# Half groups of weight matmuls moved into waiting places, two products laid side by side in 64 output rows, and one set of scores formed on VectorE

## The chip, the cores and the metric
The kernel runs on one core of one Trainium2 chip (trn2), in one launch. The metric is device microseconds. Everything is float32. Each `matmul` of the program is two MATMUL records in the trace and each transpose one, so a row that says x8 on PE is four matmuls or eight transposes.

## The reference, cut to what matters
One inference step of a 2-layer decoder trunk for a prompt of 256 tokens and 8 sample tokens that share all weights. Each layer has a mixer of three branches, merged by gates, and then a feed-forward part:

```python
z = h @ w_in                                   # one wide input projection
# branch A: gated DeltaNet in 2 chunks of 128;  branch C: mLSTM, same chunks
# branch B: latent attention
c_kv = rmsnorm(b_ckv, mla_kv_norm_g)           # latent of the newest tokens
k_rope = rope(b_kr, pos)                       # rotary key: x*cos + swapped x*(+-sin)
k_nope = einsum('bsc,chd->bshd', c_kv, w_uk)   # prompt keys of 8 heads
q_lat = einsum('bqhd,chd->bqhc', q_nope, w_uk) # sample queries in latent space
s_past = q_lat . lat_past + q_rope . kr_past   # against 2048 cached tokens a sample
s_new  = q_lat . c_kv     + q_rope . k_rope    # against the newest token: 8 samples x 8 heads
merged = g_a*(o_a @ w_branch_a) + g_b*(o_b @ w_branch_b) + g_c*(o_c @ w_branch_c)
x += merged @ w_out;   x += down(silu(conv(gate)) * up)
```

## The kernel before
Activations stay in SBUF as 128 channels x 264 tokens (256 prompt + 8 sample). Weights stream from HBM through a ring of 8 slots (SyncE issues the loads; a slot holds 8 tiles of 128x128). Nearly all of TensorE's time is `weights()` (line 546): one 128x128 tile times 264 columns. The five engines run their own written-out instruction lists and meet through semaphores.

The order on TensorE is written by hand. Some weight products depend on little and can be done at any time; these are cut into **half groups** (4 tiles, 8 records) and `half(n)` in each engine's list says "the next n half groups stand here". TensorE multiplies them (they are "fill"), ScalarE or VectorE reads each finished product at its own `half`. `PIECES` holds the 96 half groups of a layer in a fixed order: `pm` (mLSTM inputs), `pa` (latent, rotary key, latent query), `ga` gates, `wa` branch A, `gc` gates, `wc` branch C and `gb`. What isn't used up in the mixer stands in one block near its end. `schedule()` repeats the order for the PSUM banks: two banks turn among half groups, six among everything else, and `claim()` waits until the bank's last reader is through.

The places that the change touches, in the order of a layer:
- `bcL`, `bcB` (lines 650, 629): matmuls with 2 or 4 rows that spread one row over 128 partitions; VectorE reads each (1677, 1685, 1686). Then `kT` (664) and `aq` (669).
- `vn0`, `s1`, `o0`, `ks`, `vn1`, `o1`, `s2`: the DeltaNet state of the two chunks. The rotary key is product `pa` 1; its weight tile has 64 zero columns, then the key, then the key with its halves swapped.
- `bcM`, `bcI` (629), `mkT` (778), `mvT` (783), `sk` (790), `mqk` (797). From `mkT` a chain of engines follows: ScalarE copies, a table load and an Exp (1297), POOL masks (2237), VectorE multiplies (1861) and builds `vd` (1863); `outer(j)` (822) waits for that `vd` (signal `v_diag`).
- `na` (831 to 834), then `uq` (911), `uk` (923: the prompt keys, two heads in the same 64 output rows), `uv`, `ql`, `sc`.
- `sn` (978, 980): the scores of the newest tokens; then `pages(n)`: 8 samples, each 16 transposes (1005), one half group, 8 score matmuls (1012, 1015); after four, `top(g)` takes a maximum (VectorE 2011, 2013; TensorE 1028).

Of the kernel before, what the change touches and what calls it, by code (L numbers as in the profile page):

```python
# [17 lines left out]
ALU = mybir.AluOpType  # L18
# [79 lines left out]
def schedule():  # L98
# [17 lines left out]
    add("bcL", 4, "V", 4); add("bcB", 4, "V"); add("bcL", 4, "V")  # L116
# [12 lines left out]
    add("bcM", 4, "V"); add("bcI", 4, "V")  # L129
    add("mkT", 2); add("mvT", 2); add("sk", 1, "V"); add("mqk", 2, "V"); add("os", 1, "V"); half(1)  # L130
    add("mn0"); add("mc1"); half(4)
    add("out", 4, "V"); add("na"); add("out", 4, "V", 4)
# [38 lines left out]
def turn_banks():  # L171
# [32 lines left out]
    msample_kv=1, mv_diag=1, n_loaded=32, neg_max=2, next_rows=1,   # L204
# [28 lines left out]
def build(nc, a):  # L233

    with ExitStack() as ctx:
# [43 lines left out]
        td = const[:, C_LVL + 560:C_LVL + 816].rearrange("p (i n) -> p i n", i=8)  # L279
        two_step, by_one, by_two = (const[:, C_LVL + 512 + 16 * i:C_LVL + 528 + 16 * i].rearrange("p (g n) -> p g n", g=8) for i in range(3))  # L280
# [227 lines left out]
        def _(pe):  # L508
            for l in range(L):
# [43 lines left out]

                def project(name, i, rhs, k=KT, *operands, needs=()):
                    weights(claim(name, i, *operands)[:, 0:TT], rhs, k, needs=needs).then_inc(out_ready, 1)
# [10 lines left out]
                def half(n):  # L566

                    for _ in range(n):
# [10 lines left out]
                        mm = weights(early[0][:, 0:TT], rhs, 4, first, LAST_PIECE[k])  # L579
# [74 lines left out]
                for i in range(4, 8):  # L654
                    lengths(i)
                for h in range(NH):
                    spread("bcB", h, R_B)
                for i in range(4):
                    lengths(i)
# [111 lines left out]
                for h in range(NH):  # L771
                    spread("bcM", h, R_M, 0, TP)
                for h in range(NH):
                    spread("bcI", h, R_INT, P - NB, TT)
                for c_ in range(NCH):
# [12 lines left out]
                for n in range(NB):  # L788
                    for h in range(NH):
                        mm = nc.tensor.matmul(b[32 * h:32 * h + 32, 0:P], windows[:, h, 32 * n:32 * n + 32], S[:, h * NB + n, :],  # L790
                                              start=(n == 0), stop=(n == NB - 1), skip_group_check=True)
# [24 lines left out]
                half(4)  # L816
# [9 lines left out]
                for j in range(4):  # L826
                    outer(j)
                pe.wait_ge(*at(l, "oa_squares", 1))
# [7 lines left out]
                for j in range(4, 8):  # L836
                    outer(j)

# [276 lines left out]
        def _(act):  # L1115
# [19 lines left out]
            for l in range(L):  # L1135
# [95 lines left out]
                half(2)  # L1231
# [54 lines left out]
                act.wait_ge(*evac(l, "s2"))  # L1286
                for c_ in range(NCH):
# [16 lines left out]
                half(4)  # L1304
# [5 lines left out]
                A(asq[:, 1:3, :], cq, ACT.Square).then_inc(*up("oa_squares"))  # L1310
                act.wait_ge(*out(l, "na"))
                A(nrow, bank("na")[:, 0:TT], ACT.Sqrt, scale=n_scale, bias=n_bias).then_inc(*read("na"))
                act.wait_ge(*out(l, "mn1"))
# [151 lines left out]
        def _(dve):  # L1465
# [72 lines left out]
            for l in range(L):  # L1538
# [194 lines left out]
                half(3)  # L1733
# [135 lines left out]
                half(5)  # L1869
# [23 lines left out]
                half(3)  # L1893
# [85 lines left out]
                masked(1)  # L1979
                half(2)  # L1980
# [28 lines left out]
                def top(g):  # L2009
# [3 lines left out]
                    tt_(rmax[0:32, g:g + 1], rmax[0:32, g:g + 1], snew[:, g:g + 1], ALU.max).then_inc(*up("page_max"))  # L2013
                    dve.wait_ge(*out(l, "mxT", g))
# [29 lines left out]
                half(1)  # L2044
                top(0)
# [9 lines left out]
                half(2)  # L2055
                top(1)
# [424 lines left out]
```

## Time and profile before
| | |
|---|---|
| time, median of 3 runs | 1306.99 us (1306.63 to 1307.66) |
| the profiled execution's own time | 1302.87 us |
| its span in the trace | 1300.7 us |
| TensorE busy | 1278.8 us, 98% of the span |
| VectorE, ScalarE, GpSimd busy | 544.2, 253.4, 153.5 us |
| mean granted clock of TensorE | 0.992 |

The profiled execution is 4.12 us shorter than the median of the timed ones. Its first layer's mixer runs from about 12 to 410 us, the second's from about 651 to 1055 us. A matmul's end is modelled in this profile and lies some tenths of a microsecond behind the next one's start, so a busy share near 100% can still hold short waits; the starts show them.

### The profile page before, as it was taken

Reading aid. Unit: us, or ns where it says so; the run is one execution under the profiler, and the core shown is the slowest. Engines: PE = TensorE matmul, PEld = TensorE weight load, DVE = VectorE, ACT = ScalarE, POOL = GpSimd, SP = SyncE. Lnnn points to the kernel's source line nnn. Section 1 sums busy time; section 2 is a strip of 40 time slices with the busy share of each in tenths; the row PEclk is TensorE's granted clock in tenths of the full one; section 3 lists DMA queues with packets and bytes.
Section 4 is the critical chain, followed back from the end, with each engine's and each line's share of the span. In section 5 each row is a group of like instructions: output and inputs, shape, how many; then the busy total and the mean of one; then the engine's idle time right before and its main releaser. Section 6 shows DMA issues by size and latency. Waiting matters only on the chain.

```text
span 1300.7 us, 18321 instructions
## 1 busy us (share of the span) xinstructions
PE 1278.8 (98%) x7326; PEld 1047.6 (81%) x7326; DVE 544.2 (42%) x1360; ACT 253.4 (19%) x640; POOL 153.5 (12%) x210
## 2 busy tenths in 40 slices
PE   7999999999999999999999999999999999999997
PEld 6878777768888888888888787786788888888885
DVE  7874745231135333321277836533311353333212
ACT  3432424221000111110034232341210001111000
POOL 2012441200000000010001125402000000000000
PEclk9999999999999999999999999999999999999999
DMA  9423475613454444464444235645134444444440
GB/s 338 158 84 100 131 253 200 226 50 99 146 151 146 146 146 146 148 219 152 148 156 136 89 99 191 218 164 205 59 114 146 151 146 146 146 147 150 155 138 34
DMA packets 59604, 194.32 MB, mean 149 GB/s; under 512 B 7824, under 2 KB 8112, under 8 KB 56704
## 3 DMA queue, kind: packets, MB, share of 16 engines
q1 hardware_dynamic: 50544, 152.22, 36.2%
q0 software_dynamic: 8768, 40.84, 8.8%
q8 instruction: 59, 0.97, 0.3%
q14 instruction: 25, 0.20, 0.0%
q10 hardware_dynamic: 208, 0.09, 0.0%
HBM read 183.86 MB, written 9.25 MB: 148 GB/s over the span
## 4 chain that ended last, share of the span: by engine, by line
PE 95%; DVE 4%; issue 1%; ACT 1%; DMA 0%; SPq 0%; DVEq 0%; ACTq 0%
PE banks L546 75%; PE banks L1005 2%; PE banks L1012 1%; PE banks L911 1%; PE banks L1051 1%; PE banks L1015 1%; PE banks L669 1%; PE banks L629 1%; PE banks L822 1%; PE banks L923 1%; DVE arena L1627 1%; PE banks L938 1%; PE banks L790 0%; PE banks L954 0%; DMA arena<-in_x 0%
## 5 line engine op out<-in xcount | busy, mean ns | idle before, releaser
L546 PE MATMUL banks<-arena 128*128 128x264 f32 x4544 | 1035.4, 387 | 7.4 <-DVE arena L1522 6.7
L546 PEld LDWEIGHTS banks<-arena 128*128 128x128 f32 x4544 | 856.4, 190 | 167.3 <-issue 10.8
L1140 ACT ACTIVATE arena<-banks 128x256 f32<-128x256 f32 (+10 forms) x252 | 95.9, 404 | 416.7 <-PE banks L546 281.9
L2108 DVE TENSOR_SCALAR arena<-arena 128x256 f32<-128x256 f32 x44 | 18.2, 414 | 130.3 <-ACT arena L1140 130.0
L2141 DVE SCALAR_TENSOR_TENSOR arena<-banks,arena 128x264 f32<-128x264 f32 x16 | 6.9, 433 | 135.3 <-PE banks L546 135.3
L2318 POOL COPY arena<-arena 128x2 f32<-128x2 f32 x44 | 13.7, 311 | 377.6 <-ACT arena L1140 275.9
L1171 ACT ACTIVATE arena<-banks 128x264 f32<-128x264 f32 x32 | 12.6, 392 | 126.1 <-PE banks L546 126.1
L1714 DVE SCALAR_TENSOR_TENSOR arena<-arena,banks 128x264 f32<-128x264 f32 x16 | 6.9, 430 | 65.7 <-PE banks L546 65.7
L1005 PEld LDWEIGHTS banks<-arena 128*128 128x128 f32 x256 | 29.1, 146 | 6.0 <-issue 6.0
L1005 PE MATMUL banks<-arena 128*128 128x128 f32 x256 | 32.4, 281 | 0.0
L1448 ACT ACTIVATE arena<-arena 128x256 f32<-128x256 f32 x44 | 18.4, 418 | 66.4 <-DVE arena L2110 66.3
L2314 POOL DMA_DIRECT2D arena<-in_ffn x2 | 2.9, 1434 | 238.3 <-ACT arena L1140 238.3
L2115 DVE SCALAR_TENSOR_TENSOR arena<-arena 128x256 f32<-128x256 f32 x44 | 18.7, 426 | 26.3 <-ACT arena L1448 26.3
L2120 DVE TENSOR_TENSOR arena<-arena,banks 128x256 f32<-128x256 f32 x42 | 17.7, 422 | 26.7 <-PE banks L546 26.6
L2006 DVE COPY arena<-banks 128x512 f32<-128x512 f32 x32 | 21.5, 680 | 14.4 <-PE banks L1005 13.9
L2292 POOL DMA_INDIRECT arena<-in_lat,page_row x16 | 15.4, 963 | 92.1 <-ACT arena L1140 70.7
L1709 DVE SCALAR_TENSOR_TENSOR arena<-arena,banks 128x264 f32<-128x264 f32 x16 | 6.9, 430 | 42.4 <-PE banks L546 42.4
L1627 DVE SCALAR_TENSOR_TENSOR arena<-arena 128x256 f32<-128x256 f32 x48 | 23.3, 486 | 1.7
L2110 DVE SCALAR_TENSOR_TENSOR arena<-arena 128x256 f32<-128x256 f32 x44 | 21.6, 490 | 1.6
L2109 DVE SCALAR_TENSOR_TENSOR arena<-arena 128x256 f32<-128x256 f32 x44 | 21.4, 485 | 1.5
L2077 DVE SCALAR_TENSOR_TENSOR arena<-banks,arena 128x264 f32<-128x264 f32 x16 | 6.9, 433 | 34.9 <-PE banks L546 34.9
L2217 POOL TENSOR_TENSOR arena<-arena 128x512 f32<-128x512 f32 x16 | 16.1, 1037 | 37.2 <-DVE arena L1780 37.2
(429 smaller groups left out, 1085.6 us busy)
## 6 DMA issues: line engine op xcount, KB each, us to landing
arena<-in_weights SPq DMA_DIRECT2D x230, 512.0 KB, 3.5
arena<-in_weights SPq DMA_DIRECT2D x112, 256.0 KB, 3.0
arena<-in_s POOLq DMA_DIRECT2D x2, 2048.0 KB, 12.1
out_ss_o<-arena POOLq DMA_DIRECT2D x16, 256.0 KB, 3.0
arena<-in_mla_w POOLq DMA_DIRECT2D x4, 1024.0 KB, 7.3
arena<-in_c POOLq DMA_DIRECT2D x4, 512.0 KB, 5.9
out_sc_o<-arena POOLq DMA_DIRECT2D x16, 128.0 KB, 3.5
arena<-in_x SPq DMA_DIRECT2D x4, 264.0 KB, 5.0
```

The source lines that it names most:

```text
L546: mm = nc.tensor.matmul(dst, ring[:, at_:at_ + 128], rhs[:, j, :], start=(start and j == 0), stop=(stop and j == k - 1))
L1005: mm = nc.tensor.transpose(b[:, q * P:(q + 1) * P], lat[n][:, r_ * P:(r_ + 1) * P], ident)
L1140: return A(dst, src, ACT.Copy, scale=scale)
L1448: A(fth[:, j % 3, :], fcv[:, j % 3, :], ACT.Tanh, scale=0.5).then_inc(*up("ffn_tanh"))
L1627: link(stt(cv, ci[:, j, 24 + t:24 + t + TP], w[t], cv, ALU.mult, ALU.add))
L2006: V.tensor_copy(ltt[:, n % 2, i, :], bank("ltr", 4 * n + i)).then_inc(*read("ltr", 4 * n + i))
L2108: link(ts(cv, fc[:, j % 3, 0:TP], w[0], par[:, Q_FB + j:Q_FB + j + 1], ALU.mult, ALU.add))
L2109: link(stt(cv, fc[:, j % 3, 1:1 + TP], w[1], cv, ALU.mult, ALU.add))
L2110: stt(cv, fc[:, j % 3, 2:2 + TP], w[2], cv, ALU.mult, ALU.add).then_inc(*up("ffn_conv"))
L2115: link(stt(cv, fth[:, j % 3, :], 1.0, cv, ALU.add, ALU.mult))
L2120: tt_(hid[:, j, 0:TP], cv, bank("fu", j)[:, 0:TP], ALU.mult)
L2217: tt_(S[:, 4 * j:4 * j + 4, :], S[:, 4 * j:4 * j + 4, :], egl[:, j // 2, 1 + 4 * (j % 2):5 + 4 * (j % 2)].unsqueeze(2).to_broadcast((P, 4, ...
```

## The change
`schedule()` and all engines' lists: one half group more after `bcL` 4 to 7, after `bcB`, after `bcM` and after `bcI`; the four behind `mc1` become two, with one after `out` 3 and one after `out` 7; so four fewer in the last block (24 become 20). `pa` 1 and `uk` write 64 output rows each, two matmuls side by side (rows 0 to 63 and 64 to 127). VectorE forms the products for `sn` and TensorE only sums them. In `sk` the order of the samples is turned by one for each head. VectorE's half groups in `top` stand behind the maximum.

```diff
 def schedule():
     add("l2"); half(2)
-    add("bcL", 4, "V", 4); add("bcB", 4, "V"); add("bcL", 4, "V")
+    add("bcL", 4, "V", 4); half(1); add("bcB", 4, "V"); half(1); add("bcL", 4, "V")
...
-    add("bcM", 4, "V"); add("bcI", 4, "V")
+    add("bcM", 4, "V"); half(1); add("bcI", 4, "V"); half(1)
...
-    add("mn0"); add("mc1"); half(4)
-    add("out", 4, "V"); add("na"); add("out", 4, "V", 4)
+    add("mn0"); add("mc1"); half(2)
+    add("out", 4, "V"); half(1); add("na"); add("out", 4, "V", 4); half(1)
...
 # TensorE: pa 1
+                def key_weights(b, rhs, start, stop):
+                    for j in range(4):
+                        unit, part = divmod(l * UNITS * 8 + tile[0], 8)
...
+                        s = 64 * (j % 2)
+                        mm = nc.tensor.matmul(b[s:s + 64, 0:TT], ring[:, at_ + 64:at_ + 128], rhs[:, j, :],
+                                              start=(start and j < 2), stop=(stop and j >= 2), skip_group_check=True)
...
 # TensorE: sk
-                for n in range(NB):
+                for m in range(NB):
                     for h in range(NH):
+                        n = (m + h) % NB
...
 # TensorE: uk
-                        mm = nc.tensor.matmul(b[0:64, j * TP:(j + 1) * TP], wuk[:, 2 * i + j, :], ckn[:, 0:TP], start=True, stop=True)
+                        mm = nc.tensor.matmul(b[64 * j:64 * j + 64, 0:TP], wuk[:, 2 * i + j, :], ckn[:, 0:TP],
+                                              start=True, stop=True, skip_group_check=True)
...
 # TensorE: sn
-                pe.wait_ge(*at(l, "query_blocks", 1))
-                b = claim("sn", 0, ("ql", 0))
-                for n in range(NB):
-                    g, s_ = divmod(n, 4)
-                    nc.tensor.matmul(b[0:32, g:g + 1], ql_pad[:, g, s_, :], ckn[:, TP + n:TP + n + 1],
-                                     start=(s_ == 0), stop=False, skip_group_check=True)
-                    mm = nc.tensor.matmul(b[0:32, g:g + 1], qr_pad[64:96, 2, g, s_, :], kr[64:96, TP + n:TP + n + 1],
-                                          start=False, stop=(s_ == 3), skip_group_check=True)
+                pe.wait_ge(*at(l, "new_products", 1))
+                b = claim("sn")
+                for g in range(2):
+                    nc.tensor.matmul(b[0:32, g:g + 1], lat_new[:, 32 * g:32 * g + 32], ones[:, 0:1],
+                                     start=True, stop=False, skip_group_check=True)
+                    mm = nc.tensor.matmul(b[0:32, g:g + 1], key_new[:, 32 * g:32 * g + 32], ones[64:96, 0:1],
+                                          start=False, stop=True, skip_group_check=True)
...
 # ScalarE: uk
-                    copy(kf[0:64, 2 * i:2 * i + 2, 0:TP], heads(bank("uk", i)[0:64], TP)).then_inc(*read("uk", i))
+                    copy(kf[0:64, 2 * i, 0:TP], bank("uk", i)[0:64, 0:TP])
+                    copy(kf[0:64, 2 * i + 1, 0:TP], bank("uk", i)[64:128, 0:TP]).then_inc(*read("uk", i))
...
 # VectorE: pa 1
-                    r0, r1 = rot[64:96, 0:TT], rot[64:96, TT:2 * TT]
-                    tt_(r0, b[96:128, 0:TT], rope[96:128, :], ALU.mult)
-                    link(tt_(r1, b[64:96, 0:TT], rope[64:96, :], ALU.mult))
+                    r0, r1, both = rot[64:96, 0:TT], rot[64:96, TT:2 * TT], rot[64:128, 0:TT]
+                    link(V.tensor_copy(both, b[0:64, 0:TT]))
+                    link(tt_(both, both, b[64:128, 0:TT], ALU.add))
+                    tt_(r1, rot[96:128, 0:TT], rope[96:128, :], ALU.mult)
+                    link(tt_(r0, r0, rope[64:96, :], ALU.mult))
...
 # VectorE: behind masked(1): 4 products, then the signal new_products
+                for g in range(2):
...
+                last.then_inc(*up("new_products"))
...
 # VectorE: the maximum over the pages
-                def top(g):
+                def top(g, n):
...
                     tt_(rmax[0:32, g:g + 1], rmax[0:32, g:g + 1], snew[:, g:g + 1], ALU.max).then_inc(*up("page_max"))
+                    half(n)
...
-                half(1)
-                top(0)
+                top(0, 1)
```

**TensorE, the spreading matmuls.** TensorE's list in a layer behind the squared lengths (`l2`), before; L650 is `bcL`, L629 `bcB`, L664 `kT`, L669 `aq`, L546 fill:

```order
L546 MATMUL banks<-arena 128x264 x8
L650 MATMUL banks<-arena 128x264 x4
L629 MATMUL banks<-arena 128x264 x4
L650 MATMUL banks<-arena 128x264 x4
L664 MATMUL banks<-arena 128x128 x8
L669 MATMUL banks<-arena 128x256 x8
```

and after the change, where the same lines are L547, L670, L649, L686 and L691:

```order
L547 MATMUL banks<-arena 128x264 x8
L670 MATMUL banks<-arena 128x264 x4
L547 MATMUL banks<-arena 128x264 x4
L649 MATMUL banks<-arena 128x264 x4
L547 MATMUL banks<-arena 128x264 x4
L670 MATMUL banks<-arena 128x264 x4
L686 MATMUL banks<-arena 128x128 x8
L691 MATMUL banks<-arena 128x256 x8
```

A half group now stands on each side of `bcB`.

**TensorE, between the DeltaNet state and the outer products.** Behind `s2`, before; L629 is `bcM` and `bcI`, L778 `mkT`, L783 `mvT`, L790 `sk`, L797 `mqk`, L802 `os`, L808 `mn0`, L813 `mc1`, L822 `out` 0 to 3:

```order
L629 MATMUL banks<-arena 128x256 x4
L629 MATMUL banks<-arena 128x144 x4
L778 MATMUL banks<-arena 128x128 x4
L783 MATMUL banks<-arena 128x128 x8
L790 MATMUL banks<-arena 32x128 x32
L797 MATMUL banks<-arena 128x128 x8
L802 MATMUL banks<-arena 128x32
L546 MATMUL banks<-arena 128x264 x4
L808 MATMUL banks<-arena 128x128 x4
L813 MATMUL banks<-arena 64x129 x4
L546 MATMUL banks<-arena 128x264 x16
```

and after:

```order
L649 MATMUL banks<-arena 128x256 x4
L547 MATMUL banks<-arena 128x264 x4
L649 MATMUL banks<-arena 128x144 x4
L547 MATMUL banks<-arena 128x264 x4
L802 MATMUL banks<-arena 128x128 x4
L807 MATMUL banks<-arena 128x128 x8
L815 MATMUL banks<-arena 32x128 x32
L822 MATMUL banks<-arena 128x128 x8
L827 MATMUL banks<-arena 128x32
L547 MATMUL banks<-arena 128x264 x4
L833 MATMUL banks<-arena 128x128 x4
L838 MATMUL banks<-arena 64x129 x4
```

Two half groups moved up to `bcM` and `bcI`; of the four behind `mc1` two are left, so from `s2` to `out` 0 there are five as before.

**VectorE, the end of the fourth page.** L2006 copies turned pages, L1709 reads a `wa` product, L2011 and L2013 are the maximum. Before:

```order
L2003 STREAM_TRANSPOSE arena<-arena 128x512
L2006 COPY arena<-banks 128x512 x2
L1709 SCALAR_TENSOR_TENSOR arena<-arena,banks 128x264 x2
L2011 TENSOR_REDUCE arena<-banks 128x1
L2013 TENSOR_TENSOR arena<-arena 32x1
```

after:

```order
L2047 STREAM_TRANSPOSE arena<-arena 128x512
L2050 COPY arena<-banks 128x512 x2
L2055 TENSOR_REDUCE arena<-banks 128x1
L2057 TENSOR_TENSOR arena<-arena 32x1
L2060 TENSOR_REDUCE arena<-banks 1x32
```

No `wa` product stands ahead of the maximum any more: all eight have been read by then.

## Rows read from the trace of the kernel before

**Rows 1.** The page: busy time, share of the span and instructions.
```profile
PE 1278.8 (98%) x7326; PEld 1047.6 (81%) x7326; DVE 544.2 (42%) x1360; ACT 253.4 (19%) x640; POOL 153.5 (12%) x210
```

**Rows 2.** Stretches: length, busy time by engine, granted clock, DMA share, GB/s.
```profile
719.48:722.88 3.40, 3.40 (x10) 2.69 (x9) 2.53 (x7) 1.94 (x8) 0.00 (x0) 0.50 0.00 0
774.10:780.90 6.80, 6.79 (x75) 5.81 (x78) 3.61 (x25) 5.07 (x12) 0.27 (x1) 0.50 0.20 57
883.32:886.72 3.40, 3.40 (x18) 2.92 (x18) 1.34 (x4) 0.60 (x1) 2.49 (x4) 0.50 0.80 260
135.80:139.20 3.40, 3.40 (x54) 2.89 (x56) 1.54 (x12) 3.37 (x9) 0.00 (x0) 0.50 0.01 2
```

**Rows 3.** Chain that ended last: start us, length us, what (records).
```profile
75.94 0.76 PE banks L650 x8
...
79.83 1.02 PE banks L664 x8
80.85 3.48 PE banks L669 x16
...
93.38 10.88 PE banks L546 x48
...
230.05 1.78 PE banks L546 x8
...
719.56 5.14 PE banks L669 x16
```

**Rows 4.** The chain at `bcN`, two rounds of spreading matmuls.
```profile
166.08 1.09 PE banks L857 x12
```

**Rows 5.** Timeline, first layer: start, length, engine, line, shapes, records, [idle before].
```profile
131.52 0.94 PE L629 MATMUL banks<-arena 4*128 4x256 f32 x10
132.81 1.54 PE L629 MATMUL banks<-arena 4*128 4x144 f32 x6 [0.35 <-DVE arena L1824]
134.96 1.75 ACT L1140 ACTIVATE arena<-banks,arena 128x64 f32<-128x64 f32 x8 [3.62 <-PE banks L778]
137.71 1.28 ACT L1297 ACT_TABLE_LOAD   x1
140.15 1.99 POOL L2237 TENSOR_TENSOR arena<-arena 128x1024 f32<-128x1024 f32 x1 [6.17 <-ACT arena L1297]
142.18 1.29 DVE L1861 TENSOR_TENSOR arena<-arena,banks 128x512 f32<-128x512 f32 x2 [1.85 <-POOL arena L2237]
143.38 4.67 DVE L1863 TENSOR_TENSOR arena<-arena 128x1024 f32<-128x1024 f32 x1
152.59 1.99 PE L822 MATMUL banks<-arena 32*128 32x512 f32 x8
```

**Rows 6.** Timeline, second layer, the same two ends.
```profile
771.90 0.94 PE L629 MATMUL banks<-arena 4*128 4x256 f32 x10
793.94 1.99 PE L822 MATMUL banks<-arena 32*128 32x512 f32 x8
```

**Rows 7.** Timeline: `sk` and, in the same form, `mq`.
```profile
136.74 3.13 PE L790 MATMUL banks<-arena 128*32 128x128 f32 x64
```

**Rows 8.** The chain: `mq`, `uk`, `pv` pairs, `sn`.
```profile
178.69 1.97 PE banks L879 x64
...
198.11 3.60 PE banks L923 x16
...
232.20 0.22 PE banks L964 x4
...
239.84 0.15 PE banks L978 x2
```

**Rows 9.** Who waited for whom: total us, times, longest.
```profile
PE banks L1028 <- DVE arena L2013: 2.8, 2, 1.4
```

**Rows 10.** Timeline of the DeltaNet inverse: its last step and TensorE's start on it.
```profile
103.21 0.62 DVE L1778 STREAM_TRANSPOSE arena<-arena 128x256 f32<-128x256 f32 x1
...
104.19 0.69 PE L682 MATMUL banks<-arena 32*32 32x32 f32 x32
```

More of the change, by code:

```diff
@@ L279, in build @@
         td = const[:, C_LVL + 560:C_LVL + 816].rearrange("p (i n) -> p i n", i=8)
+        lat_new, key_new = const[:, C_LVL:C_LVL + 64], const[64:96, C_LVL + 64:C_LVL + 128]
         two_step, by_one, by_two = (const[:, C_LVL + 512 + 16 * i:C_LVL + 528 + 16 * i].rearrange("p (g n) -> p g n", g=8) for i in range(3))
@@ L552, in weights @@
                     return mm
+                def key_weights(b, rhs, start, stop):
+                    for j in range(4):
+                        unit, part = divmod(l * UNITS * 8 + tile[0], 8)
+                        slot = unit % SLOTS
+                        if part == 0:
+                            pe.wait_ge(w_landed[slot], landed[unit])
+                        at_ = slot * 1024 + part * 128
+                        s = 64 * (j % 2)
+                        mm = nc.tensor.matmul(b[s:s + 64, 0:TT], ring[:, at_ + 64:at_ + 128], rhs[:, j, :],
+                                              start=(start and j < 2), stop=(stop and j >= 2), skip_group_check=True)
+                        if part == 0:
+                            mm.then_inc(w_started, 1)
+                        tile[0] += 1
+                    return mm
                 def project(name, i, rhs, k=KT, *operands, needs=()):
@@ L578, in half @@
                         rhs = oa if name == "wa" else oc if name == "wc" else hn if first else hn[:, 4:8, :]
-                        mm = weights(early[0][:, 0:TT], rhs, 4, first, LAST_PIECE[k])
+                        if (name, i) == ("pa", 1):
+                            mm = key_weights(early[0], rhs, first, LAST_PIECE[k])
+                        else:
+                            mm = weights(early[0][:, 0:TT], rhs, 4, first, LAST_PIECE[k])
                         if LAST_PIECE[k]:
@@ L655, in _ @@
                     lengths(i)
+                half(1)
                 for h in range(NH):
                     spread("bcB", h, R_B)
+                half(1)
                 for i in range(4):
@@ L772, in _ @@
                     spread("bcM", h, R_M, 0, TP)
+                half(1)
                 for h in range(NH):
                     spread("bcI", h, R_INT, P - NB, TT)
+                half(1)
                 for c_ in range(NCH):
@@ L815, in _ @@
                 mm.then_inc(out_ready, 1)
-                half(4)
+                half(2)
                 def outer(j):
@@ L827, in _ @@
                     outer(j)
+                half(1)
                 pe.wait_ge(*at(l, "oa_squares", 1))
@@ L837, in _ @@
                     outer(j)
+                half(1)
                 b = claim("mn1", 0, ("mqk", 1), ("mc1", 0))
@@ L1230, in _ @@
                 A(l2row, bank("l2")[:, 0:TT], ACT.Sqrt, scale=l2_scale, bias=l2_bias).then_inc(*read("l2"))
-                half(2)
+                half(4)
                 act.wait_ge(*at(l, "rows_dve", 1))
@@ L1286, in _ @@
                 act.wait_ge(*evac(l, "s2"))
+                half(2)
                 for c_ in range(NCH):
@@ L1303, in _ @@
                 copy(c1, pair).then_inc(*read("mc1"))
-                half(4)
+                half(2)
                 act.wait_ge(*evac(l, "os"))
@@ L1310, in _ @@
                 A(asq[:, 1:3, :], cq, ACT.Square).then_inc(*up("oa_squares"))
+                half(1)
                 act.wait_ge(*out(l, "na"))
                 A(nrow, bank("na")[:, 0:TT], ACT.Sqrt, scale=n_scale, bias=n_bias).then_inc(*read("na"))
+                half(1)
                 act.wait_ge(*out(l, "mn1"))
@@ L1731, in half @@
                                 early_wc(i)
-                half(3)
+                half(5)
                 dve.wait_ge(*at(l, "conv_state", 1))
@@ L1868, in _ @@
                 V.tensor_copy(windows[:, :, 0:232:33], mq[:, :, TP:TT])
-                half(5)
+                half(6)
                 dve.wait_ge(*at(l, "s_decayed", 8))
@@ L1892, in _ @@
                 last.then_inc(*read("mc2"))
-                half(3)
+                half(4)
                 dve.wait_ge(*at(l, "oa_scaled", 1))
@@ L2054, in _ @@
                 pages(7)
-                half(2)
-                top(1)
+                top(1, 2)
                 half(4)
```

13 lines of the change are left out of this document (11 added, 2 removed).

## The prediction
> **What bounds the kernel now.** I read the page first: TensorE is busy for 98% of the span and no other engine for half of it [rows 1]. So only three things can shorten this kernel: less work on TensorE, less waiting on TensorE that the modelled ends of its matmuls hide, and a higher clock. I therefore read starts, not busy shares, in the mixer of each layer, and then the granted clock of each stretch.
>
> The clock: four stretches, 17.0 us together, have a granted clock of 0.50 [rows 2], the lower of the two levels (1.2 GHz), while the mean of the span is 0.992, so nearly all else runs at the upper one (2.4 GHz). Ahead of three of them TensorE had been waiting at the spreading matmuls (`bcL`/`bcB` in layer 2; `bcM`/`bcI` in both layers), ahead of the fourth it ran the tiny `sn` matmuls. What the level costs is seen on `aq`: 8 matmuls take 3.48 us in layer 1 and 5.14 us in layer 2 [rows 3].
>
> The waits: six spreading matmuls in two rounds, with nothing to wait for, take 1.09 us [rows 4], 0.55 a round of up to four. But from the first `bcL` at 75.94 to `aq` at 80.85 [rows 3] are 4.91 us for three such rounds and `kT`: VectorE reads banks in between. From `bcM` at 131.52 to the copies of `mkT` at 134.96 are 3.44 us for two rounds and a bit, with VectorE named as what ended the wait [rows 5]. And at the first maximum over the pages TensorE waits 1.4 us in each layer for VectorE [rows 9].
>
> **The unit.** A half group alone is 1.78 us (230.05 in [rows 3]). Behind a spreading matmul, 24 matmuls took 10.88 us, that is six halves of 1.78 and 0.20 [rows 3]. So a half group put among the spreading matmuls costs 1.98. Every half group moved up is taken from the last block, where it cost 1.78.
>
> The Trainium skill ("TensorEngine Tiling (Array Packing)", Key Properties) says that changing the tiling mode drains TensorE, and this speaks against the change, which puts 128-row weights between matmuls of 4 or 2 rows. The 0.20 above agrees. Without drains, as its "up to 2x" for 64 columns would have it, the key product below would give 3.5 us in both layers together rather than 2.2, and the sum would be 1.3 us larger; I stay with the row.
>
> **Part 1, the halves at `bcL`/`bcB`.** After: round 0.76 (as at 75.94), fill 1.98, round 0.55, fill 1.98, round 0.55, `kT` 1.02: 6.84 us against 4.91. VectorE reads four banks in each fill; the 4.91 us held three such rounds of reading, so one takes under 1.7 us, within the 1.98, and no wait is left. 3.56 us of fill has been placed for 1.93 us: gain 1.63 a layer, 3.3 us in both. In layer 2 the low clock ahead of `aq` should go too: 5.14 - 3.48 = 1.7 us. Behind it, VectorE's inverse ends at 103.83 and TensorE starts on it at 104.19 [rows 10]; only 0.36 us are free there, but both are moved later by the same 1.93 us and the number of halves between is the same, so I cost it at nothing; had VectorE been moved by more, each microsecond over 0.36 would be lost.
>
> **Part 2, the halves at `bcM`/`bcI`.** Here the chain of engines behind `mkT` becomes the limit. Before, in layer 1: ScalarE starts on `mkT` at 134.96, table load at 137.71, POOL 140.15, VectorE 142.18, `vd` 143.38 to 148.05 [rows 5], 13.1 us in all, while TensorE reaches `out` 0 only at 152.59: 4.5 us of slack. After: 0.55 for `bcM`, 1.98, 0.43 for `bcI`, 1.98, 0.25 until the first `mkT` is out, 0.25 for ScalarE to finish the half group's copy: 5.4 us behind 131.52, or 137.0. `v_diag` comes at 137.0 + 13.1 = 150.1, and as TensorE has two halves fewer behind `mc1`, it waits for it: first at `mn0` (whose `pt` comes at 142.18 + 0.65 + 2.0 = 144.9 while TensorE is there near 143), then barely at `out` 0. Five halves stand in the stretch before and after, so the gain is 152.59 - 150.1 = 2.5 us in layer 1. In layer 2 the same steps from 771.90 give 790.4 against 793.94 [rows 6]: 3.5 us, more since 6.8 us there were at the low clock. Together 6.0 us, the clock in it. What is queued behind the wait on TensorE (`out`, `na`) is waited for by ScalarE and VectorE, which are on no path until `bcN`, 13 us later.
>
> `sk` takes 3.13 us, while `mq`, which has the same form, takes 1.97 [rows 7, 8]. The first is inside a stretch at 0.50, the second is not, so the difference is the clock, and the turned order of `sk` is costed at nothing. Bounds: 0 to 1.2 us a layer if it were the addresses; but that stretch is hidden behind the chain above either way.
>
> The halves around `na` add two changes of form a layer, 0.3 us: minus 0.6.
>
> **Part 3, the rotary key side by side.** Two matmuls with 64 output rows run at once: a `pv` pair of 128 columns takes 0.22 [rows 8], what one matmul of 128x128 takes (`kT`: 8 transposes of one record in 1.02, [rows 3], and a matmul has two). So 8 matmuls of `pa` 1 become four pairs, 3.56 to 1.78, less about 0.35 for each of the two halves to change form there and back (0.15 in, 0.20 out): 1.1 a layer, 2.2. Bounds: 0 (no overlap) to 3.5. The halves are now around `vn0`, where 0.9 us instead of 1.8 must cover a copy of ScalarE's of 128x512; no row shows it uncovered, and I take it as covered, with 0.5 us a layer as the other bound. VectorE's two added operations have `s1` and `o0` to hide behind.
>
> **Part 4, prompt keys side by side.** `uk`: 3.60 us for 8 matmuls [rows 8], already of 64 rows, so no new change of form: half of it, 1.75 a layer, 3.5. ScalarE gets 8 copies for 4; what waits for the last of them is `sc`, behind `uv` and `ql`. Bounds 0 to 3.6.
>
> **Part 5, `sn`.** 16 matmuls at 0.15 us (two records: 0.15, [rows 8]) become 4: 1.8 a layer, 3.6. VectorE's four products stand behind `masked(1)`, tens of microseconds ahead of `sn`. The low clock in layer 2 behind it (3.4 us, at which TensorE does half) gives 1.5, the part of it that overlaps work.
>
> **Part 6, `top`.** VectorE no longer waits for a `wa` product ahead of the maximum: 1.4 in each layer [rows 9], 2.8.
>
> **Sum.** 3.3 + 1.7 + 6.0 - 0.6 + 2.2 + 3.5 + 3.6 + 1.5 + 2.8 = 24.0 us. From the profiled execution's own 1302.87 that is 1278.9. The median of the timed runs is 4.12 us above that execution. With the difference carried over it would be 1283.0. I choose the middle, 1281: layer 1 passes two places at the full clock that layer 2 doesn't, and timed runs that don't are a likely part of the 4.12 us, which would then go as well.
>
> **Rivals.**
> - *The waits are a fiction.* TensorE idles for only 22 us by the page [rows 1]; if the moved halves earn nothing but the removed work stays, parts 3 to 6 without the clock: 12.1 us, 1294 to 1295. Against it: the starts and VectorE as releaser [rows 5]. Chance 0.08.
> - *The clock falls elsewhere.* The wait at `mn0` (some 1.9 us) comes behind spreading matmuls, and the side-by-side pairs give TensorE less to do. Two to four new stretches, about 1.7 us each as for `aq`: 1285 to 1289. Chance 0.15.
> - *The pairs don't overlap.* Parts 3 and 4 fall away: 5.7 us, 1287. Against it the `pv` row. Chance 0.04.
> - *More is won.* The whole 4.12 us goes, and the chain of part 2 starts earlier than I count: 1272 to 1276. Chance 0.13.
> - *Slower.* Weights come too late: in each mixer four half groups, 1 MB, are asked for up to 7 us earlier, beside the state loads (the stretch at 883.32 has a DMA share of 0.80 [rows 2]). SyncE would be late and TensorE wait in `weights()`. It decides only from 24 us of waiting on, 12 a layer; the ring holds 16 half groups, 28 us. Chance 0.02.
>
> The forecast itself has 0.58, with 1276 to 1287 as its own range. The range that leaves out no more than two in ten is 1273 to 1290. What a measurement of this kernel can tell from no change is about 0.2%, 2.6 us; all cases but the last are faster by more. Faster 0.96, same 0.02, slower 0.02.
>
> **What would show it.** `bcL` to `aq` about 6.8 us in both layers and `aq` 3.5; no stretch at 0.50 in the mixers; `bcM` to `out` 0 about 18.5 us with a wait at `mn0`; each `pa` 1 half about 0.9 to 1.2 us; `uk` 1.8; `sn` 0.6; no wait at line 1055 (the maximum's transpose). Wrong would make it: a wait on the inverse, a wait at `s1`, new low stretches, or a wait on weights.

## The result, and the profile after

The changed kernel takes 1289.35 us (median of 4 runs, 1288.2 to 1290.15) against 1307.12 for the kernel before in the same runs (1306.63 to 1307.66): a ratio of 0.986, 95% interval 0.985 to 0.988, or 17.8 us less. The forecast was 1281 us with a range of 1273 to 1290: the sign was right, and the time lies inside the range by 0.65 us. The two profiled executions differ less: 1302.87 us before and 1288.2 after, 14.7 us (14.4 in the span), where the sum of the prediction had 24.0. So two questions stand: where 9.6 us of the sum went, and why the timed runs gained 3 us more than the profiled ones. Of all executions below, one of products_only was far slower (1909.22 us at a granted clock of 0.651) and has no part in its ratio.

The page of the changed kernel, its line of busy times (compare [rows 1]):
```profile
span 1286.3 us, 18245 instructions
PE 1259.2 (98%) x7278; PEld 1027.6 (80%) x7278; DVE 546.0 (42%) x1372; ACT 254.3 (20%) x648; POOL 153.1 (12%) x210
```
TensorE is still busy for 98%, with 19.6 us less work. Now the places that the prediction named. First the chain, as in [rows 3], from `bcL` to `aq` in layer 1, then `aq` of layer 2, the two halves of the key around `vn0`, `uk`, `sn`, pages 0 and 1, and the maximum's transpose:
```profile
76.28 0.73 PE banks L670 x8
77.00 1.98 PE banks L547 x8
78.98 0.66 PE banks L649 x8
79.64 1.98 PE banks L547 x8
81.62 0.66 PE banks L670 x8
82.27 1.02 PE banks L686 x8
83.30 3.47 PE banks L691 x16
...
716.15 3.47 PE banks L691 x16
...
119.60 1.04 PE banks L564 x8
120.64 1.09 PE banks L761 x8
121.73 1.04 PE banks L564 x8
...
200.99 1.96 PE banks L950 x16
...
241.11 0.15 PE banks L1005 x2
...
246.97 0.86 PE banks L1042 x8
247.83 1.90 PE banks L1032 x16
249.73 1.95 PE banks L547 x8
251.68 0.02 issue
251.70 0.60 ACT arena L1167
252.30 1.57 another core or an unknown queue
253.87 0.02 issue
253.89 0.61 ACT arena L1167
254.49 0.73 issue
255.22 1.09 PE banks L1039 x8
...
270.26 0.11 PE banks L1055
```
Each row is start, length, what; the rows from 246.97 to 255.22 are for later. `bcL` to `aq` is 83.30 - 76.28 = 7.02 us, with two half groups inside, and a half group behind a spreading matmul takes exactly the 1.98 of the prediction. `aq` takes 3.47 in both layers, where layer 2 had 5.14. A half group of the key takes 1.04 instead of 1.78, `uk` 1.96 instead of 3.60, and the maximum's transpose follows its half group at once.

The timeline from `bcM` to `out` in layer 1, and two copies at page 1 (compare [rows 5]; in brackets the idle time before, and who ended it):
```profile
132.77 0.71 PE L649 MATMUL banks<-arena 4*128 4x256 f32 x8
133.41 2.05 PE L547 MATMUL banks<-arena 128*128 128x264 f32 x8
...
139.14 1.97 PE L815 MATMUL banks<-arena 128*32 128x128 f32 x64
...
143.45 1.99 POOL L2280 TENSOR_TENSOR arena<-arena 128x1024 f32<-128x1024 f32 x1 [8.22 <-ACT arena L1325]
145.47 1.29 DVE L1894 TENSOR_TENSOR arena<-arena,banks 128x512 f32<-128x512 f32 x2 [3.93 <-POOL arena L2280]
146.31 1.13 PE L833 MATMUL banks<-arena 128*128 128x128 f32 x8 [1.22 <-DVE arena L1894]
146.68 4.66 DVE L1896 TENSOR_TENSOR arena<-arena 128x1024 f32<-128x1024 f32 x1
...
151.72 1.56 PE L847 MATMUL banks<-arena 32*128 32x512 f32 x6
...
251.70 0.60 ACT L1167 ACTIVATE arena<-banks 128x512 f32<-128x512 f32 x1 [7.34 <-PE banks L547]
253.83 1.29 DVE L2050 COPY arena<-banks 128x512 f32<-128x512 f32 x2 [6.79 <-remote]
```
It takes 18.95 us from 132.77 to the first `out` at 151.72 instead of 21.07 in [rows 5], and TensorE waits 1.22 us at `mn0` for VectorE, as forecast. `sk` takes 1.97 us, as `mq` does.

And now what the prediction did not have. Who waited for whom, first for TensorE as a whole, in us, times and longest:
```profile
PE banks L1039 <- ACT arena L1167: 6.9, 2, 3.7
```
The place is page 1. In the chain above TensorE finished its 16 transposes (line 1032, from 247.83) and a half group by 251.68. ScalarE had nothing else to do and should have copied the first four transposes at about 248.5; it began at 251.70, and VectorE at 253.83 (the last two rows of the timeline). The kernel has one core, so "remote" and "another core" mean that the profile found nobody. The trace's semaphore records show what was missing: TensorE's updates, most of which come 0.01 us behind the modelled end of the instruction, came up to 5 us late. The one of page 0's scores came at 249.53 instead of 247.83, those of the four groups of transposes at 251.68, 253.81, 253.87 and 253.92 instead of 248.42 to 249.73. TensorE then waited 3.7 us for copies that had waited for its own updates.

In layer 2 it was 3.2 us, and behind it stands the only stretch at the lower clock before the kernel's end. Windows, as in [rows 2]: two of the wait in layer 1, and that stretch:
```profile
250.00:252.00 2.00, 1.52 (x7) 0.95 (x5) 0.00 (x0) 0.30 (x1) 1.70 (x2) 1.00 1.00 410
252.00:254.00 2.00, 0.00 (x0) 0.00 (x0) 0.17 (x1) 0.41 (x2) 0.09 (x1) 1.00 1.03 428
...
888.34:891.75 3.41, 3.41 (x19) 1.61 (x12) 0.06 (x1) 0.19 (x1) 0.00 (x0) 0.50 1.00 414
```
What else ran then: GpSimd issued the gathers of pages 4 to 7, eight indirect transfers at a pitch of 1.25 us, from 242.3 to 251.1, behind the fourth `pv`. The kernel before does the same from 241.1. But there page 0's transposes start 1.6 us behind the first of these gathers, and here 0.1 us ahead of it, since `sn` between them is 1.8 us shorter.

### The profile page after: what moved, and what is told of

Read it like the earlier page. It is cut to its first block, busy times and chain, and to the rows that moved or that the text cites. A ratio compares the mean times of both kernels' runs of the same rounds, so it can differ in the third digit from the quotient of the medians.

```text
span 1286.3 us, 18245 instructions
## 1 busy us (share of the span) xinstructions
PE 1259.2 (98%) x7278; PEld 1027.6 (80%) x7278; DVE 546.0 (42%) x1372; ACT 254.3 (20%) x648; POOL 153.1 (12%) x210
## 4 chain that ended last, share of the span: by engine, by line
PE 93%; DVE 3%; issue 2%; ACT 1%; POOL 0%; DMA 0%; another core or an unknown queue 0%; ACTq 0%; DVEq 0%; POOLq 0%
PE banks L547 75%; PE banks L1032 2%; PE banks L1039 1%; PE banks L1042 1%; PE banks L938 1%; PE banks L1078 1%; PE banks L847 1%; DVE arena L1658 1%; PE banks L966 1%; PE banks L691 1%; PE banks L982 0%; PE banks L564 0%; DMA arena<-in_par 0%; POOL arena L2280 0%; PE banks L906 0%
## 5 line engine op out<-in xcount | busy, mean ns | idle before, releaser
L547 PE MATMUL banks<-arena 128*128 128x264 f32 x4512 | 1031.3, 388 | 7.5 <-DVE arena L1553 6.8
L547 PEld LDWEIGHTS banks<-arena 128*128 128x128 f32 x4512 | 850.3, 190 | 171.6 <-issue 15.9
L1167 ACT ACTIVATE arena<-banks 128x256 f32<-128x256 f32 (+8 forms) x260 | 96.9, 396 | 436.0 <-PE banks L547 300.8
L1747 DVE SCALAR_TENSOR_TENSOR arena<-arena,banks 128x264 f32<-128x264 f32 x16 | 6.9, 430 | 73.6 <-PE banks L547 73.6
L1039 PE MATMUL banks<-arena 128*32 128x512 f32 x128 | 17.6, 618 | 7.3 <-ACT arena L1167 6.9
```

Source lines behind the costliest of these rows:

```text
L547: mm = nc.tensor.matmul(dst, ring[:, at_:at_ + 128], rhs[:, j, :], start=(start and j == 0), stop=(stop and j == k - 1))
L1039: nc.tensor.matmul(heads(sb[32 * i:32 * i + 32, :], 32), ql_pad[:, g, s_, :], turned_lat(n)[:, :, 32 * i:32 * i + 32], start=(s_ == 0), st ...
L1167: return A(dst, src, ACT.Copy, scale=scale)
```

## The experiments

Times are medians; the kernel before had 1308.0, 1309.2 and 1309.4 in the three series. Spans and waits are those of each kernel's profiled execution.

### First series: the gathers, and parts of the change alone

**late_gathers**, on the changed kernel:
```diff
-                pool.wait_ge(*evac(l, "pv", 3))
+                pool.wait_ge(*evac(l, "ltr", 7))
                 plain()
                 for n in range(4, NB):
                     gather(n)
```


> The changed kernel with one wait moved: POOL issues the gathers of pages 4 to 7 after the last copy of page 1's transposes, no longer after the fourth pv. Theory A (the burst of these gathers, which in the changed kernel coincides with the transposes of page 1, makes TensorE's semaphore updates arrive late): the 3.7 and 3.2 us of waiting in page 1 go, and the low clock behind the second (1.7) with them, 8 us in all: about 1281. If the lateness goes along with the burst, it shows at a later page, and the gain is smaller. Pages 4 to 7 are transposed some 20 us after page 1, and the four gathers took 10 to 12 us, so no wait for data is expected. Theory B (the lateness comes from the weight load issued beside page 1, or from the half groups there): the wait stays at page 1 and the time at 1289.

Measured 1282.94 us (1282.44 to 1283.95), ratio 0.982 (0.980 to 0.983). The waits at page 1 are gone, and so is every low stretch before the kernel's end. The lateness went along with the burst, now from 252.5 to 261.3, but smaller: 1.5 us in each layer at page 3.
```profile
PE banks L1039 <- ACT arena L1198: 3.0, 2, 1.5
```
8 us less these 3.0 would be 1284.4, and 1282.9 came out. Theory A stands; B, which had 1289, is out.

**sn_matmuls**, on the changed kernel (the removed lines of `sn` return, VectorE's products go):
```diff
+                for n in range(NB):
+                    g, s_ = divmod(n, 4)
+                    nc.tensor.matmul(b[0:32, g:g + 1], ql_pad[:, g, s_, :], ckn[:, TP + n:TP + n + 1],
...
```


> The changed kernel with the newest-token scores back as 16 matmuls. It costs TensorE 1.8 us a layer. Theory A: the gathers then start 1.8 us earlier against TensorE's stream, as they do before, and the waits in page 1 (3.7 and 3.2) and the low clock (1.7) go: 1289.4 + 3.6 - 6.9 - 1.7 = 1284.4. Theory B (the wait has nothing to do with the gathers' place): the waits stay, 1293.

Measured 1287.12 us (1286.75 to 1287.5): with 3.6 us more work on TensorE the kernel is 2.2 us faster. The direction is A's, the size isn't: from 1284.4 there are 2.7 us missing. The trace has 2.0 us of lateness left at page 1 of layer 1 (0.4 ahead of its transposes, 1.6 between them and the scores), 0.4 in layer 2, and a low stretch at 876.9.

**products_only**, on the kernel before (only `sn` changed):
```diff
+                pe.wait_ge(*at(l, "new_products", 1))
+                b = claim("sn")
+                for g in range(2):
+                    nc.tensor.matmul(b[0:32, g:g + 1], lat_new[:, 32 * g:32 * g + 32], ones[:, 0:1],
...
```


> The kernel before with the newest-token scores alone multiplied on VectorE. It saves 1.8 us a layer, 3.6. Theory A: the gathers fall 1.8 us later against TensorE's stream and the wait in page 1 appears in one or both layers, so that the time is 1307 - 3.6 + up to 6.9 = 1304 to 1310. Theory B: no wait in page 1, and 1307 - 3.6 = 1303.4, or 1301.9 if a low clock behind the 16 matmuls goes too.

Measured 1307.13 us against 1308.02, ratio 1.0005 (0.999 to 1.002): no difference clear of the noise, though 3.6 us of work are gone. The wait has appeared at page 1 in both layers, 3.1 us each, with the same mark in the chain:
```profile
249.00 1.59 PE banks L1005 x12
250.60 0.02 issue
250.62 0.60 ACT arena L1140
251.22 3.63 another core or an unknown queue
```
So this one part of the change makes the wait, without the moved half groups and without the pairs.

**halves_only**, on the kernel before (`schedule()`; the other lists likewise):
```diff
-    add("bcL", 4, "V", 4); add("bcB", 4, "V"); add("bcL", 4, "V")
+    add("bcL", 4, "V", 4); half(1); add("bcB", 4, "V"); half(1); add("bcL", 4, "V")
...
-    add("bcM", 4, "V"); add("bcI", 4, "V")
+    add("bcM", 4, "V"); half(1); add("bcI", 4, "V"); half(1)
...
-    add("mn0"); add("mc1"); half(4)
-    add("out", 4, "V"); add("na"); add("out", 4, "V", 4)
+    add("mn0"); add("mc1"); half(2)
+    add("out", 4, "V"); half(1); add("na"); add("out", 4, "V", 4); half(1)
```


> The kernel before with the half groups alone moved (2 into bcL and bcB, 2 into bcM and bcI, 2 from mc1 to around na). By the trace of the changed kernel: 2.9 at bcL, 1.7 for the low clock ahead of aq, 5.0 at bcM, less 0.4 at na: 9.2 us, so 1298. Theory A: no wait in page 1, since pv to page 1 stands as before. Theory B (the half groups that stand beside page 1, four places further in the list, and the weight load that they start, make the wait): it shows here too, and the time is 1305 to 1307.

Measured 1294.24 us (1293.11 to 1296.73), ratio 0.991 (0.989 to 0.993): more than expected. The span is 1291.0 us, 9.7 less than before, although page 1 holds 0.4 and 2.0 us of lateness. What the expectation missed stands in the chain at the maximum:
```profile
271.12 1.98 PE banks L546 x8
273.10 0.11 PE banks L1034
```
The 1.4 us of [rows 9] are gone, without any edit in `top`. Four half groups were moved up, so the one beside the maximum is no longer `wa` 6 (number 54 of `PIECES`), which VectorE must read first, but `gc` 1 (number 58), which ScalarE reads. The 2.8 us that the prediction gave to part 6 belong to the moved half groups.

This kernel also settles `sk`: its order of samples is the old one, its clock is full, and it takes 1.97 us.
```profile
140.27 1.97 PE L794 MATMUL banks<-arena 128*32 128x128 f32 x64
```
The 3.13 of [rows 7] was the clock.

### Second series: what belongs to the lateness, and a better place

**late_load**, on the changed kernel:
```diff
                 if u >= SLOTS:
                     sp.wait_ge(w_started, u - SLOTS + 2)
+                if u % UNITS == 51:
+                    sp.wait_ge(*at(u // UNITS, "lat_in7", 32))
```


> The changed kernel, in which SyncE holds back one load of a weight unit (512 KB), the one that is asked for beside pages 0 and 1, until the gather of page 7 has landed. Theory A1 (the gathers alone make TensorE's semaphore updates late): the waits at page 1 (3.7 and 3.2 us) stay, and the time with them, 1289. Theory A2 (it takes the gathers and the weight load together): the waits go, and the low clock too, 1282 to 1283. The ring holds enough for the delay of some 12 us, so no wait for weights is expected.

Measured 1288.65 us (1287.73 to 1289.89), waits of 3.2 us in both layers. In the trace the load is issued at 258.4 in layer 1, where the changed kernel has 244.6. So the weight load is not needed for the lateness: A1.
```profile
PE banks L1041 <- ACT arena L1169: 6.4, 2, 3.2
```

**spread_gathers**, on the changed kernel:
```diff
-                pool.wait_ge(*evac(l, "pv", 3))
-                plain()
                 for n in range(4, NB):
+                    pool.wait_ge(*(evac(l, "pv", 3) if n == 4 else evac(l, "ltr", 4 * n - 17)))
+                    plain()
                     gather(n)
```


> The changed kernel with the gathers of pages 4 to 7 spread: page 4's after the fourth pv as in the changed kernel, then one pair of gathers after the last copy of page 0's, 1's and 2's transposes. Theory A1 (a long burst of gathers makes the updates late): a pair takes about 2.5 us to issue and 4 to 5 us to land, at a pitch of 5.6 us, so the DMA share stays below 1 and neither page 1 nor page 3 waits: 1281 to 1282, at least as fast as the gathers moved as a whole (1282.9). If it is each gather by itself that disturbs, each page waits a little, 1 to 1.5 us, and the time is 1286 to 1290.

Measured 1279.74 us (1279.27 to 1280.68), ratio 0.978 (0.975 to 0.980): 9.6 us faster than the changed kernel. The pages follow one another without a gap:
```profile
246.09 1.02 PE banks L1039 x8
247.11 0.86 PE banks L1042 x8
247.97 1.90 PE banks L1032 x16
249.87 1.79 PE banks L547 x8
251.66 1.02 PE banks L1039 x8
```
Transposes to scores is 3.69 us, its length wherever nothing is late.

**before_late**, on the kernel before: the edit of late_gathers.
```diff
-                pool.wait_ge(*evac(l, "pv", 3))
+                pool.wait_ge(*evac(l, "ltr", 7))
```


> The kernel before with the same one wait moved (gathers of pages 4 to 7 after the last copy of page 1's transposes). The kernel before has no wait at page 1. If late gathers are worth something only because the change put a wait there, this is no faster, and with the 1.5 us of waiting at page 3 of each layer that the changed kernel showed with it, 1307 to 1311 less up to 1.7 for the low clock at page 0 of layer 2. If they were worth 6 us by themselves, 1301.

Measured 1310.5 us against 1309.19, ratio 1.001 (0.999 to 1.002): no gain, with 1.7 us at page 3 of each layer. The same edit that gave the changed kernel 6.4 us gives this one nothing. Its profiled execution also had more stretches at the low clock than that of the kernel before, mean 0.989 against 0.992.

**pairs_only**, on the kernel before (the key through `key_weights`, and `uk`):
```diff
+                        if (name, i) == ("pa", 1):
+                            mm = key_weights(early[0], rhs, first, LAST_PIECE[k])
...
-                        mm = nc.tensor.matmul(b[0:64, j * TP:(j + 1) * TP], wuk[:, 2 * i + j, :], ckn[:, 0:TP], start=True, stop=True)
+                        mm = nc.tensor.matmul(b[64 * j:64 * j + 64, 0:TP], wuk[:, 2 * i + j, :], ckn[:, 0:TP],
...
```


> The kernel before with the rotary key and the prompt keys side by side alone. By the trace of the changed kernel 1.2 and 1.6 us a layer: 5.7 us, 1301.5 to 1302 on a median of 1307.5. The fourth pv and the first page's transposes both come earlier by the same, so the gathers keep their place and no wait at page 1 is expected (theory A1 and A2). A theory that the wait came with the pairs (less work of TensorE ahead of the pages, any removal at all) expects it here: 1305 to 1308.

Measured 1302.25 us (1300.03 to 1303.84), ratio 0.995 (0.994 to 0.997). The gain is there, but "no wait" was wrong: the trace has 2.1 us of lateness at page 1 of layer 1 and 0.6 in layer 2, with the gathers 1.6 and 2.1 us ahead of page 0, just as in the kernel before, which had none.

### Third series: more of the cause, and the best version

**spread_fill**, spread_gathers and one more half group ahead of `mn0` (the other lists likewise):
```diff
-    ... add("os", 1, "V"); half(1)
+    ... add("os", 1, "V"); half(2)
```


> The changed kernel with the gathers spread, and one more half group ahead of the first mn0, taken from the last block. The wait of 1.2 us there in each layer is filled: a half group of 1.98 goes in for 1.78 at the end, so 1.0 us a layer is won if the outer products can start 0.8 us later without loss: 1279.7 - 2.0 = 1277.7. If the end of VectorE's product (v_diag) sets the start of the outer products, as it does by the wait of 0.3 us there, the later start costs part of it: 1278.5. If it starts a low clock anew: 1281.

Measured 1276.78 us (1276.63 to 1276.94), ratio 0.975 (0.974 to 0.976), the fastest of all. The wait at `mn0` is filled, and nothing waits at `out`:
```profile
143.00 3.81 PE L547 MATMUL banks<-arena 128*128 128x264 f32 x16
146.64 1.05 PE L833 MATMUL banks<-arena 128*128 128x128 f32 x8
...
151.98 1.99 PE L847 MATMUL banks<-arena 32*128 32x512 f32 x8
```
From `bcM` to the first `out` it is 19.27 us (132.71 to 151.98) where spread_gathers has 18.95: a half group for 0.3 us that cost 1.78 in the last block, 1.5 a layer, 3.0 in all. I had expected 2.0. I counted one more change of form, but the added half group stands behind another one and takes 1.78 (3.81 for two, where one alone took 2.03). So `mn0` starts only 0.38 us later (13.93 us behind `bcM`, against 13.55 in spread_gathers), not 0.8, and from there to the first `out` it is 5.34 us against 5.40.

**spread_sn**, spread_gathers with `sn` as 16 matmuls again (the edit of sn_matmuls):
```diff
+                for n in range(NB):
+                    g, s_ = divmod(n, 4)
...
```


> The changed kernel with the gathers spread and the newest-token scores back as 16 matmuls. Where the gathers were in a burst, these 16 matmuls made it 2 us faster. If that was only their 1.8 us of delay against the burst, here they cost their own 3.6 us: 1279.7 + 3.6 = 1283.3, or 1285 if a low clock comes back behind them. If they have a good of their own: 1278 to 1280.

Measured 1284.74 us (1284.59 to 1285.41): 5.0 us slower than spread_gathers. 3.6 of that are matmuls; 1.4 remain, and a stretch at 0.50 is back behind them, at 875.0. The same edit that won 2.2 us beside the burst loses 5.0 without it. That is part 5 of the prediction, both of its terms.

**before_spread**, on the kernel before: the edit of spread_gathers.
```diff
+                    pool.wait_ge(*(evac(l, "pv", 3) if n == 4 else evac(l, "ltr", 4 * n - 17)))
```


> The kernel before with the gathers of pages 4 to 7 spread, all else as before. Its profiled execution had no wait at page 1 and took 1302.9, while its timed runs had 1305.5 to 1312. Theory A3 (the timed runs of the kernel before do wait at page 1 or 2 in many executions, since it stands at the edge, 1.6 us from where the changed kernel lost 3.7): now 1302 to 1303 and with less scatter. If the scatter has another cause, 1307 to 1308 and as wide as before.

Measured 1305.29 us (9 runs, 1304.14 to 1307.08) against 1309.36 for the kernel before in the same series (14 runs, 1306.12 to 1311.09), ratio 0.9975 (0.996 to 0.9985). The scatter falls from 5.0 to 2.9 us and the median by 4.1, to 1305.3, not to 1303. The granted clocks of the timed runs divide this. At 0.991, the kernel before took 1306.1 to 1306.5 us (three runs) and this one 1304.1 to 1305.0 (three); at 0.988 it was 1308.3 to 1310.1 (four) against 1305.9 to 1307.0 (three). So at an equal clock some 2 us go with the burst. The rest goes with the clock: four runs of the kernel before had only 0.985 or 0.986 (1310.2 to 1311.1 us), and none of the nine here. That the 2 us were waiting at page 1 or 2 is likely and not shown, since the profiled execution of the kernel before had no such wait.

**keys_early**, on the changed kernel:
```diff
+                for n in range(4, NB):
+                    gather(n, ("key",))
                 pool.wait_ge(*evac(l, "pv", 3))
                 plain()
                 for n in range(4, NB):
-                    gather(n)
+                    gather(n, ("lat",))
```


> The changed kernel with the four key gathers of pages 4 to 7 taken out of the burst and issued behind those of page 3, some 40 us earlier; the four big gathers of the burst are then issued in 5 us and not in 10. If it is the bytes that queue up (each big gather is 1 MB, each key gather 256 KB), the wait at page 1 stays at 3 us or grows, 1288 to 1291. If it is the number of gathers or the time that GpSimd spends on issuing them, it halves, 1284 to 1286.

Measured 1279.99 us (1279.59 to 1280.35), ratio 0.978 (0.976 to 0.979): no page waits any more. Both branches of my expectation are wrong in size, and the first altogether, for the DMA engines are as full as ever. Windows of keys_early, to be set beside those of the changed kernel above:
```profile
246.00:248.00 2.00, 2.00 (x20) 0.64 (x18) 1.05 (x2) 0.00 (x0) 1.49 (x2) 1.00 1.01 410
252.00:254.00 2.00, 2.00 (x18) 0.42 (x16) 1.05 (x2) 0.00 (x0) 0.00 (x0) 1.00 1.02 426
```
A DMA share of 1.0 and more than 400 GB/s leave TensorE at 2.00 of 2.00 us here, and at 0.00 from 252 to 254 there. What differs at the pages is that four gathers are issued in a row instead of eight.

But this edit has a second effect, which I had not thought of: the four key gathers now stand behind those of pages 2 and 3, so eight are issued in a row there, from 204.6 to 214.4. And there the updates are late again. Those due at 212.07 and 212.52 came at 213.77 and 214.51, the next one, due at 214.51, at 216.03, and in layer 2 it is the same. ScalarE shows the mark:
```profile
213.80 0.39 ACT L1194 ACTIVATE arena<-banks 128x264 f32<-128x264 f32 x1 [4.70 <-remote]
```
TensorE waits for nobody there, so it costs nothing. keys_early has moved the lateness out of the way, as late_gathers did, and not removed it.

## Why the prediction was right or wrong

**The sum, by its parts** (both layers; "measured" is from the chains of the two profiled executions, or as said):

| part | predicted | measured |
|---|---|---|
| 1, halves at `bcL` | 3.3 | 2.9 (7.02, not 6.84, for 4.91) |
| 1, low clock ahead of `aq` | 1.7 | 1.7 |
| 2, halves at `bcM` | 6.0 | 5.2 (2.12 and 3.10) |
| 2, halves around `na` | -0.6 | -0.4 |
| 3, key side by side | 2.2 | 2.4 |
| 4, prompt keys | 3.5 | 3.3 |
| 5, `sn` | 3.6 | 3.6 |
| 5, low clock behind it | 1.5 | about 0; 1.4 with the gathers spread |
| 6, maximum | 2.8 | 2.8, but from the moved halves |
| waits at page 1 | 0 | -6.9 |
| sum | 24.0 | 14.6 (spans: 14.4) |

The step that failed is in part 5: "16 matmuls at 0.15 us (two records: 0.15, [rows 8]) become 4: 1.8 a layer, 3.6", with nothing said of what `sn` keeps apart. The matmuls were priced rightly and are gone. But they had stood between the fourth `pv`, which releases eight gathers, and the pages, whose transposes ScalarE and VectorE must copy within 3.69 us if TensorE is not to wait. The sum has no term for such a wait; the runs show 6.9 us of it. Taken alone, this part is worth nothing (products_only, 1.0005); beside the burst, undoing it is worth 2.2 us; with the gathers spread it is worth 5.0. That the time still lies inside the range is luck: the range reached to 1290 for the sake of lower clocks, not of a wait at the pages. None of the rivals had it: "The clock falls elsewhere" gave 1285 to 1289 and so came nearest to the 1289.35, but by another cause. Only one stretch of low clock is there, and it stands behind a wait.

The other terms are right within 0.8 us, part 5's clock apart. With the burst taken apart, the changed kernel takes 1279.74 us and its profiled span is 22.8 us below that of before. That is the prediction's sum less 1.2, of which the smaller gain at `bcM` is 0.8.

**Part 2** was short by 0.8. The chain of engines behind `mkT` is as long as I took it, and the wait at `mn0` is there. But `mn0` starts 13.54 us behind `bcM` (132.77 to 146.31), where I had 13.4, and from `mn0` TensorE needs another 5.41 for `mn0`, `mc1` and two half groups. That is when the first `out` starts, 151.72, and not the end of `vd` at 151.34. The prediction had named both and let `vd` set the time (18.6 us behind `bcM`, against 18.95 measured), without adding up TensorE's own work behind `mn0`. **Part 6** had the right size and the wrong owner (halves_only). The Trainium skill's rule on changing the tiling mode ("TensorEngine Tiling (Array Packing)", Key Properties), which I had weighed against the 0.20 of [rows 3], agrees with the trace once more: each half group of the key stands behind another form and takes 1.04 us, not 0.89, the half of 1.78.

**The 4.12 us** between profiled and timed runs of before: I carried half of it over, on the thought that timed runs meet more low clock. 3.1 of it went (17.8 measured against 14.7 between the profiled executions), 1.15 remains. The reason was at best a part of it. before_spread brings the kernel before down by 4.1 us, some 2 of them at an equal granted clock and the rest by the clock. No trace was taken of an execution of the kernel before that lost these, so where they were lost stays open.

**What the lateness depends on.** Lateness at page 1 by the place of the burst, layer 1 and layer 2 ("lead" is from the issue of the first gather to the first transpose of page 0; lateness is transposes to scores, less 3.69):

| kernel | lead, us | late, us |
|---|---|---|
| before | 1.6, 2.1 | 0, 0 |
| pairs_only | 1.6, 2.1 | 2.1, 0.6 |
| halves_only | 2.1, 1.7 | 0.4, 2.0 |
| sn_matmuls | 1.6, 1.7 | 1.6, 0.4 |
| changed | -0.1, -0.1 | 3.8, 3.2 |
| products_only | -0.1, -0.1 | 3.1, 3.1 |
| late_load | -0.1, -0.1 | 3.3, 3.2 |

At a lead of -0.1 all six cases lose 3.1 to 3.8 us; at 1.6 to 2.1 the eight cases lose 0 to 2.1, in no order of the lead. So the change went from a place where the burst costs something now and then to one where it cost 3 us in each of the six layers seen.

Shown: wherever TensorE's updates were more than 1 us late, eight gathers were being issued in a row or had just been. late_gathers and keys_early move the lateness with the eight, and spread_gathers, spread_sn and spread_fill, which have no eight in a row, have no update over 1 us late. The weight load is not needed (late_load). Eight in a row are not enough (the kernel before), and full DMA engines aren't either (the kernel before, keys_early at the pages). Nor do bytes decide: in keys_early the eight gathers with late updates are two of 1 MB and six of 256 KB, 3.5 MB, and the four without are 4 MB. Open: by what path gathers hold up TensorE's semaphore updates, and whether it is their number, their small key packets (the four without late updates had no key gather among them), or GpSimd's ten microseconds of issuing.

## What to carry to other kernels

Work that is taken from between two others also takes away their distance: for every removed instruction, ask which transfer its predecessor releases and what that will now run beside, not only who waits for the instruction. When an engine's copy starts microseconds behind the matmul that it waits for and the profile names nobody, look at which gathers are being issued, and spread them, one page's pair per page, before blaming either engine. Look also where a moved gather lands: keys_early took four out of one burst and made another with them. And test a part both in and out of its surroundings: the same 16 matmuls were worth 0, -2.2 and +5.0 us in three of them.

## What the runs showed of the hardware that I had not expected

- In the changed kernel TensorE's semaphore updates came 1.7 to 5.0 us behind their instructions while eight gathers were issued in a row. At the pages of keys_early, with four in a row and 410 to 426 GB/s in the windows shown, they came 0.01 to 0.18 us behind, and up to 2.0 us in layer 1 where eight stood in a row, from 204.6 on. In the profiled execution of the kernel before they came at most 0.04 behind at the pages, with eight.
- The wait of 3.2 us at page 1 in layer 2 was followed at once by 3.4 us at a granted clock of 0.50, in the changed kernel and in late_load; the longer one in layer 1 was not in either, nor were the two of products_only.
- Each of the seven kernels with the 16 one-column matmuls of `sn` (2.4 us of them) has one stretch at 0.50 at page 0, 3.4 us long, in one of its layers: at 883.3 in the kernel before, 876.9 in sn_matmuls, 246.2 in halves_only, 889.0, 880.2, 875.0 and 244.6 in before_late, pairs_only, spread_sn and before_spread. None of those with the 4 matmuls has one there.
